# Two-layer diffusion trunk: when the last three query/key tiles get their norms and low halves, and where group A's outputs go

## The reference

```
q_w, k_w, v_w, q_n, k_n, v_n, q_g, k_g, v_g = split_mixer_inputs(h @ w_in, qk_g)   # RMS norm per head on every q and k
q_w, k_w = apply_rope(q_w, cos, sin), apply_rope(k_w, cos, sin)                    # A: window of 128, sink logits, 6 heads
q_g, k_g = apply_rope(q_g, cos, sin), apply_rope(k_g, cos, sin)                    # C: all keys, 6 heads
o = concatenate([window_attention(q_w, ...), neighbourhood_attention(q_n, ...), global_block_attention(q_g, ...)])
x = x + ga_a * (o @ w_out)
x = x + ga_f * swiglu(modulate(rms_norm(x, g_ffn), sh_f, sc_f), w_gate, w_up, w_down)
```

## Time and profile before

| | us |
|---|---|
| median of 3 runs | 1706.69 (1705.18 to 1708.16) |
| profiled execution, its own time | 1705.99 |
| its span | 1704.2 |
| layer 0, scores of step 0 to scores of step 12 on DVE | 208.8 to 242.0 |
| layer 1, the same | 1159.7 to 1191.4 |

### The profile page before, as it was taken

The page is one execution under the profiler, slowest core; times in us unless marked ns, Lnnn a source line. Parts: engine busy times, 40 slices in busy tenths (PEclk is TensorE's granted clock), DMA queues, the critical chain, the costliest instruction groups (busy, mean ns, idle before and its releaser), DMA issues.

```text
span 1704.2 us, 29725 instructions
## 1 busy us (share of the span) xinstructions
PE 1632.2 (96%) x11685; PEld 1120.3 (66%) x11685; DVE 1025.6 (60%) x2075; ACT 745.2 (44%) x1367; POOL 739.6 (43%) x474
## 2 busy tenths in 40 slices
PE   7999989998999999999999999997998899999998
PEld 3688878977856656666666667886887544444444
DVE  3434498884479873788358855456995526326234
ACT  4222278884144341334313323225894455355342
POOL 1244335572614443344433343550403567567563
PEclk9999999999989999999999999998999899999999
DMA  9355453323045412353326232554103242243222
GB/s 325 58 133 138 118 150 98 94 63 88 26 123 161 137 56 93 99 164 120 113 75 225 79 69 53 135 135 114 28 6 101 62 136 87 75 136 96 66 87 87
DMA packets 317290, 179.24 MB, mean 105 GB/s; under 512 B 88527, under 2 KB 310495, under 8 KB 317151
## 3 DMA queue, kind: packets, MB, share of 16 engines
q1 hardware_dynamic: 284542, 143.63, 30.6%
q10 hardware_dynamic: 32608, 33.71, 6.2%
HBM read 158.97 MB, written 2.83 MB: 95 GB/s over the span
## 4 chain that ended last, share of the span: by engine, by line
PE 73%; DVE 15%; issue 5%; ACT 3%; DMA 2%; SPq 1%; POOL 1%; ACTq 0%; DVEq 0%; POOLq 0%
PE acc L958 60%; DVE mod_acc L2148 4%; DVE prob L1930 2%; DVE prob_t L1936 2%; PE small L905 2%; PE mod_ps L1058 1%; PE side L1143 1%; PE side L895 1%; ACT prob_t L1516 1%; PE acc L1126 1%; PE acc L1127 1%; DVE mod_acc L2146 1%; ACT prob L1494 1%; DMA tokens<-in_ctx 1%; PE mod_ps L1143 1%
## 5 line engine op out<-in xcount | busy, mean ns | idle before, releaser
L958 PE MATMUL acc<-act,pair_w 128*128 128x512 f16 x3168 | 580.2, 345 | 5.6 <-ACT act L1395 3.5
L958 PEld LDWEIGHTS acc<-act,pair_w 128*128 128x128 f16 x3168 | 309.5, 99 | 265.5 <-issue 10.6
L958 PE MATMUL acc<-act,split_w 128*128 128x512 f32 (+1 forms) x1920 | 378.6, 355 | 9.3 <-DVE act L2080 4.6
L958 PEld LDWEIGHTS acc<-act,split_w 128*128 128x128 f32 x1920 | 307.7, 189 | 63.6 <-DVE act L2080 6.8
L799 POOL TENSOR_SCALAR pair_raw<-pair_raw,weight_scale 128x1024 f32<-128x1024 f32 x88 | 109.6, 1246 | 324.9 <-ACT pair_w L1566 324.9
L958 PE MATMUL acc<-hidden,down_w 128*128 128x512 f16 (+1 forms) x1056 | 247.8, 343 | 1.6 <-DVE hidden L2114 0.8
L723 POOL TENSOR_SCALAR split_w<-raw_w 128x1024 fp32r<-128x1024 f32 x72 | 77.1, 1071 | 342.9 <-PE acc L958 231.0
L2148 DVE SCALAR_TENSOR_TENSOR mod_acc<-mod_chunk,silu_c,mod_acc 128x256 f32<-128x256 f32 x280 | 198.0, 751 | 4.0
L802 POOL TENSOR_TENSOR pair_w<-pair_raw,pair_w 128x1024 f16<-128x1024 f32 x88 | 192.4, 2187 | 7.3
L726 POOL TENSOR_TENSOR split_w<-raw_w,split_w 128x1024 fp32r<-128x1024 f32 x72 | 171.9, 2388 | 6.0
L2109 DVE SCALAR_TENSOR_TENSOR prod<-acc,prod_scale,silu_g 128x768 f32<-128x768 f32 (+1 forms) x44 | 38.9, 884 | 208.0 <-PE acc L958 199.0
(11 more groups left out here) (229 smaller groups left out, 2462.8 us busy)
## 6 DMA issues: line engine op xcount, KB each, us to landing
mod_chunk<-in_w_mod ACTq DMA_DIRECT2D x28, 1024.0 KB, 5.2
pair_raw<-in_w_gate SPq DMA_DIRECT2D x44, 512.0 KB, 3.7
pair_raw<-in_w_up SPq DMA_DIRECT2D x44, 512.0 KB, 4.8
raw_w<-in_w_in SPq DMA_DIRECT2D x64, 256.0 KB, 3.8
raw_w<-in_w_mod SPq DMA_DIRECT2D x24, 512.0 KB, 4.0
raw_w<-in_w_down SPq DMA_DIRECT2D x20, 512.0 KB, 4.5
mod_start<-in_w_mod SPq DMA_DIRECT2D x8, 1024.0 KB, 11.0
ks<-q_split SPq DMA_DIRECT2D x64, 96.0 KB, 2.4
```

The source lines that it names most:

```text
L958: mm = pe.matmul(acc[slot][:, a:b], own, moving[:, part == 1, k, a:b], start=(k == 0 and part == 0), stop=(k == n - 1 and part == 1))
```

## The change

The table of positions is now per layer. Step numbers are positions in the layer's list.

| | norm 13, 14, 15 | high half 13, 14, 15 | low half 12, 13, 14, 15 |
|---|---|---|---|
| before, both layers | 2, 6, 7 | 3, 7, 8 | 1, 4, 8, 9 |
| after, layer 0 | 14, 37, 42 | 15, 38, 43 | 1, 17, 40, 45 |
| after, layer 1 | 4, 7, 9 | 5, 8, 10 | 1, 6, 9, 11 |

Within a step, DVE does the norm and the low half behind `turned_low` and no longer ahead of it. Tile 15's sums of squares and its turned row go to `small` and not to `mod_ps`, so its sums need not wait for the row of tile 14; its `inverse` moves behind the scores of step 1, its turned row behind the first transposes (PE) and to step 3 (ACT), and ACT squares it before copying it. Its copy goes to a buffer of its own, `raw_last`. In layer 0 A's outputs go to `o_a` (in the bytes of `bias`, which is filled later), and one DMA of 1152 KB moves them to `o`; SP's part of the late tiles is spread over the modulation loads.

```diff
+LATE_NORM = [{14: 13, 37: 14, 42: 15}, {4: 13, 7: 14, 9: 15}]
+LATE_HIGH = [{15: 13, 38: 14, 43: 15}, {5: 13, 8: 14, 10: 15}]
+LATE_LOW = [{1: 12, 17: 13, 40: 14, 45: 15}, {1: 12, 6: 13, 9: 14, 11: 15}]
...
+        o_a = place("o_a", [P, 6, 6 * HD], F32, a0 + 18624)
+        raw_last = place("raw_last", [P, TOK], F32, a0 + 44736)
...
+        def sums_at(j):
+            return small if j == 15 else mod_ps
+        def raw_at(j):
+            return raw_last if j == 15 else raw_q[j % 3]
...
                 if l == 0:
                     for n in range(4, len(ATTN_MOD)):
+                        if n == 6:
+                            inv_from_dram(l, 15)
+                        elif n == 7:
+                            stack_up(l, 13)
+                        elif n == 12:
+                            stack_up(l, 14)
+                        elif n == 14:
+                            stack_up(l, 15)
+                        elif n == 17:
+                            sp.wait_ge(o_ready, outputs_of_a(0))
+                            for p in range(2):
+                                sp.wait_ge(stack_in[p], 16 * stack_count(N_QK + p))
+                            sp.dma_start(o[:, :, 0:6 * HD], o_a[:, :, :]).then_inc(o_moved, 16)
                         load_mod(n)
...
-                        if i:
+                        if i and j < 15:
                             pe.wait_ge(q_row, i)
...
+                        if j == 15:
+                            sc.wait_ge(q_ssq, l * N_QK + qk_before(j) - 1)
+                            sc.activation(sq[slot][:, 0:w], acc[slot][:, 0:w], ACT.Square).then_inc(q_sq, 1)
...
+                    aside = l == 0 and s["group"] == "A"
+                    o_ = o_a if aside else o
-                    if k == 0:
+                    if k == (outputs_of_a(0) if l == 0 else 0):
                         ve.wait_ge(t_lo, N_QK * (l + 1))
...
-                    if g == g0:
+                    if g - g0 == 1:
                         inverse(15)
-                    if g - g0 in (2, 6, 7):
-                        norm_tile({2: 13, 6: 14, 7: 15}[g - g0])
-                    if g - g0 in (1, 4, 8, 9):
-                        round_low({1: 12, 4: 13, 8: 14, 9: 15}[g - g0])
                     if g0 <= g - 2 < g1:
                         turned_low(g - 2)
+                    if g - g0 in LATE_NORM[l]:
+                        norm_tile(LATE_NORM[l][g - g0])
+                    if g - g0 in LATE_LOW[l]:
+                        round_low(LATE_LOW[l][g - g0])
```

More of the change, by code:

```diff
@@ L316, in trunk @@
         wide = place("wide", [P, 4, ROWS, 48], F32, a0 + 38592)
-        mod_row = [place(f"mod_row{i}", [4, P], F32, a0 + 46784 + i * 512) for i in range(2)]
+        o_a = place("o_a", [P, 6, 6 * HD], F32, a0 + 18624)
+        raw_last = place("raw_last", [P, TOK], F32, a0 + 44736)
+        mod_row = [place(f"mod_row{i}", [4, P], F32, a0 + 47808 + i * 512) for i in range(2)]
         b0 = at[0]
@@ L1057, in after_copy @@
                             c = t
-                            mm = pe.matmul(mod_ps[:, c:c + tiles + 1:tiles], sq[slot][:, P * t:P * t + P],
+                            mm = pe.matmul(sums_at(j)[:, c:c + tiles + 1:tiles], sq[slot][:, P * t:P * t + P],
                                            pair_ones[:, 0:P:64], start=True, stop=True)
@@ L1179, in _ @@
                         weigh(g - 4)
+                    if g - g0 == 2:
+                        turn_inv(15)
                     if l == 0 and g - g0 in MOD_STEP:
@@ L1185, in _ @@
                 pe.wait_ge(o_ready, outputs_before(l) + outputs_of_a(l))
+                if l == 0:
+                    pe.wait_ge(o_moved, 16)
                 pe.wait_ge(exps, g1)
@@ L1419, in take_root @@
                         sc.wait_ge(q_inv, i - 1)
-                    sc.activation(root_tok[i % 2][:, 0:n], mod_ps[:, 0:n], ACT.Sqrt, bias=eps[:, 0:1],
+                    sc.activation(root_tok[i % 2][:, 0:n], sums_at(j)[:, 0:n], ACT.Sqrt, bias=eps[:, 0:1],
                                   scale=1.0 / HD).then_inc(q_root, 1)
@@ L1430, in take_row @@
                         sc.wait_ge(inv_out[i % 2], 16 * (i // 2))
-                    sc.activation(inv_row[i % 2][0:n, :], mod_ps[0:n, 32:32 + P], ACT.Copy).then_inc(q_row, 1)
+                    sc.activation(inv_row[i % 2][0:n, :], sums_at(j)[0:n, 32:32 + P], ACT.Copy).then_inc(q_row, 1)
                 def swap_halves(j):
@@ L1478, in _ @@
                             sc.activation(raw[:, 0:w], acc[slot][:, 0:w], ACT.Copy).then_inc(qkv_copied, 1)
-                        if kind[0] != "v":
+                        if kind[0] != "v" and j < 15:
                             if qk_before(j) >= 2:
@@ L1520, in _ @@
                 for g in range(g0, g1 + 2):
-                    if g - g0 == 2:
+                    if g - g0 == 3:
                         take_row(15)
@@ L1951, in take_outputs @@
                     ve.wait_ge(o_ps, LAYER_STEPS[l][0] + i + size)
-                    if k == 0:
+                    aside = l == 0 and s["group"] == "A"
+                    o_ = o_a if aside else o
+                    if k == (outputs_of_a(0) if l == 0 else 0):
                         ve.wait_ge(t_lo, N_QK * (l + 1))
-                    if GROUPS[l][k - 1][1] == 8 and not s["local"]:
+                    if GROUPS[l][k - 1][1] == 8 and not s["local"] and not aside:
                         for p in range(2):
```

37 lines of the change are left out of this document (21 added, 16 removed).

## The result

The changed kernel takes 1710.15 us (median of 19 runs, 1707.60 to 1711.67); the kernel before, in the same rounds, 1706.63. The ratio is 1.0022 with an interval of 1.0015 to 1.0029: slower by 3.5 us, where 5.9 less was forecast. The rival called "slower" gave 1710.2. The profiled execution has a span of 1706.6 us against 1704.2.

A forecast was written before the change was run, and what follows sets the result against it. PE was taken as the overall bound, DVE in layer 0's first steps and layer 1's attention. Layer 0's 8.6 - 6.0 = 2.6 plus layer 1's 3.3 gave 5.9 us: 1700.8 us, with 8 of 10 in 1694.5 to 1705.

The forecast's parts named there:

- slower: Rival: PE pays layer 0's arrivals in full, DVE's 15.4 us against 8.6 won; 1710.2 us, chance 0.07.
- Part 1: Layer 0, steps 0 to 12: three norms and three low halves leave DVE; gain 8.6 us, bounds 5.4 to 9.7.
- 3.2 from the clock: Layer 0, steps 0 to 12: PE work run at half speed would be about 3.2 us shorter at full speed.
- Part 2: Tile 15's sums in another bank, squared first: removes PE's 1.08 us wait once a layer, counted within Part 1 and Part 5.
- Part 3: Layer 0, steps 14 to 45: norms and low halves arriving beside a full PE lose 6.0 us, bounds 0.7 to 7.8.
- the slack: Layer 0, around the three arrival clusters: DVE lateness that PE would forgive through depth and rest, 7.6 us.
- five of six places colliding: Layer 0, new norm and low-half places: all but step 42 wait for POOL's splits, 7.1 us in sum.
- 3.1 for step 14: Layer 0, step 14: the norm's two instructions wait for POOL's two split instructions, about 3.1 us.
- the depth: Layer 0 arrivals: with three banks and two score buffers DVE can be about 1.2 us late per cluster, 3 x 1.2.
- the rest: DVE's idle time, 0.22 us a step in A and 0.42 in C, about 4.0 over eleven steps, to absorb arrivals.
- Part 4: SP's queue and the move of A's outputs: 0 us, bounds 0 to 2; product 14's split keeps 1.5 us margin.
- Part 5: Layer 1, steps 0 to 12: norm at step 4 cuts DVE's idle time of 6.12 us; gain 3.3, bounds 1.2 to 4.5.

The follow-up runs named there:

- e1: Changed kernel with layer 0's norms and low halves of tiles 13 to 15 cut to 16 columns or fewer, instructions kept: 1701.8 us, 0.9967 to the kernel before.
- e2: Changed kernel, all work kept, POOL holding six split pairs next to arrivals until DVE is past them: 1702.1 us, 0.9967 to the kernel before.
- e6: Changed kernel with the edits of e1 and e2 together: 1698.3 us, 0.9954 to the kernel before.
- e3: Changed kernel with layer 0's norms, high and low halves and SP's order at the kernel before's steps: 1704.6 us, 0.9987 to the kernel before.

## Why the prediction was wrong

**Part 1 was right**: 8.0 for 8.6, steps 0 to 12 in 25.14 for 24.6. PE is busy 24.00 of 25.10, DVE 19.40; the clock came back only to 0.93, so 0.8 of the forecast's 3.2 from the clock stayed out. **Part 2 was right**: PE waits 0.16 for ACT's squares where it stood for 1.08; PE in order of time, after:

```profile
208.29 1.63 PE L1092 MATMUL small<-pair_ones,sq 128*128 128x2 f32 x12 [0.16 <-ACT sq L1511]
```

**Part 3 is the step that failed, and in it the slack.** That norms and low halves would collide with POOL's splits was right; what PE would forgive was not. What DVE would get was forecast at 8.3 to 15.4 us and is 13.5. What stands against it was put at 7.6: "3 x 1.2 and about 4.0 of rest", of which, with the lower end of the sum mixed in, a loss of 6.0 came. Measured is 13.6. The 13.5 lies inside the forecast's bounds, but is not made up as it had it: the waits for POOL were 2.5 at step 14, 1.4 at 37 and 1.8 at 45 and none at 17, 40 and 42, 5.8 in sum, where the forecast had 7.1 with five of six places colliding. Its 3.1 for step 14 was also summed wrongly: 246.7 to 249.8 is the time from the norm's start to the end of the splits, and the norm works in part of it. By its own rows the norm would end 0.8 behind the split, at 250.6, and alone at 248.45: 2.2. Three things were off in what stood against it.

First, the depth: 0.72, 0.39 and 0.12 at the three norms, 1.2 together and not 3.6. It was argued from the length of a step and not read from a row; the low halves alone were free, where no norm stood close.

Second, the rest was not there to be spent. DVE's idle time of 0.22 or 0.42 us a step was nearly all a wait for PE's scores or for ACT's part of the probabilities (in steps 12 to 23 1.1 and 1.0 us, in steps 40 to 55 5.0 and 0.7). A delay of PE did not shrink behind an arrival: in the changed kernel the scores, counted from step 12 and against the kernel before, are 5.4 us late at every step from 18 to 24, and 5.65 at every step from 25 to 37. PE's idle time grew by 9.8 for DVE's 13.5, so 3.7 of it was forgiven in all: the depth at the three norms, and the low halves, which cost little or nothing with POOL held; not eleven steps of rest.

Third, a missing term: PE's clock. The forecast counted what the clock gives back where a stop goes (part 1) and forgot that it is taken where one arrives: 66.11 us of PE for 62.23, 3.9 us, in the changed kernel, and 0.5 with POOL held, where the clock stayed full. So 3.4 is the clock's, nearly all of it from the two falls behind steps 14 and 37, 1.6 each.

With these, 13.5 - 3.7 + 3.9 = 13.7. (This is bookkeeping: 3.7 is read from the same windows as the loss. That the loss hangs on the exclusion and the duration is shown by e1, e2 and e6.)

**The rival.** "Slower" gave 1710.2 by assuming that DVE's 15.4 is paid in full; it was to decide if over three quarters of the inserted time shows as PE's idle time. It shows as 73%, and the clock makes up the rest. By its own test, then, it did not hold. Its 1710.2 is right by luck: it forgave nothing where 3.7 was forgiven, left out the 3.9, took 15.4 for DVE's 13.5 and 11.9 for the 10.5 that steps 0 to 12 won in the two layers. At 0.07 the outcome was priced too low all the same: the argument against it, that PE idled only 6.8 us beside a DVE without rest in the first steps, was taken from a stretch where PE was busy for 26.43 us of 33.20 and so had room.

**Part 4 was right.** Load 14 was issued later than forecast (309.09 for 304.6), because DVE and with it the stack were late; the split of load 12 stood for 8.59 us on its DMA, and PE stopped for no product. The move of A's outputs is one issue of 0.67 us; e3 has it and loses nothing. SP's issues in order of time, after:

```profile
306.40 2.65 SPq L606 DMA_DIRECT2D qs<-q_split  x4
309.09 0.59 SPq L564 DMA_DIRECT2D raw_w<-in_w_mod  x1
...
318.76 0.67 SPq L687 DMA_DIRECT2D o<-o_a  x1
```

**Part 5 was right**, 2.5 for 3.3: the norm at step 4 does not wait for its DMA as it did in the earlier trace rows, and the clock there is 0.94 for 0.84. DVE in order of time at that step, after:

```profile
1173.27 0.28 DVE L1976 SCALAR_TENSOR_TENSOR prob_t<-mod_ps,prob_t 128x128 f16<-128x128 f32 x1
1173.46 0.47 DVE L1882 SCALAR_TENSOR_TENSOR q_raw<-raw_q,vecs,root 128x256 f32<-128x256 f32 x1
```

Left open: what makes the clock fall behind one stop and not behind another (1.57 and 1.91 against 1.81 at the same step); why the low half at step 18 costs 0.9 and at 17, 40 and 45 next to nothing; and what the 1.0 us that is left in e6 consists of (0.3 of it comes at step 25, 0.2 at step 38 to 39, 0.5 at steps 42 to 44).

## What to carry to other kernels

Idle time of an engine that waits for the bound engine each step is no store: take an arrival's price as its length less one small depth, read from a stop in the trace, and add what the bound engine's clock may lose behind the stop (here 1.5 to 1.6 us where it fell, nothing where it didn't). When work is moved behind an event, look at what else that event starts (here a product frees a split on POOL, and the norm was put right behind it); holding the engine that has time won 8.5 us here, more than any choice of steps that was tried. If the work must go into a full stretch, cut it in two or three: the loss fell from 7.0 to between 4.0 and 4.7 here, and a cut in four gained nothing more.

## What was not expected of the hardware

An elementwise DVE instruction of 16 columns took 0.95 and 1.71 us beside POOL's split and 0.23 without: its price there was POOL's remaining time, and not its own work. Two DVE instructions in a row waited for both halves of a POOL pair (1.21 and 3.16), but a short second one (0.22) got in between them. And PE's stops of 1.57, 1.81 and 1.91 us at the same step had 1.68, 1.12 and 1.87 us for the same 16 matmuls behind them: the shortest stop did not leave the clock at full speed, the middle one did.
